# When four of the 2 MB cache copies are issued in a decoder step with two layers: from layer B into the memory attention stage

## The reference

```python
def layer_b(h, mem_k, mem_v, w_in, conv_w, ..., w_out, conv_state, delta_state):
    proj = h @ w_in
    qkv, b, a, qm, z = jnp.split(proj, ...)
    ...                                         # conv, silu, l2norm, decay
    o, S = gated_delta(q, k, v, g, beta, S0)
    o = rmsnorm(o, o_norm_w)...
    om = mem_attend(qm, mem_k, mem_v)           # softmax over 256 memory tokens, 4 heads
    branch = jnp.concatenate([o, om], axis=-1) * jax.nn.silu(z)
    return branch @ w_out, new_conv, S

# layer A, sample group, for each of the three windows (128, 512, 2048):
kc = jnp.concatenate([kbuf, k], axis=1)
keep = min(win, L + T)
return o, lse, kc[:, L + T - keep:], vc[:, L + T - keep:]
```

## Time and profile before

| what | value |
|---|---|
| median of 3 runs | 2200.28 us (2195.5 to 2202.48) |
| the profiled execution's own time | 2194.7 us |
| its span, first to last instruction | 2192.7 us |
| PE busy | 2154.7 us, 98% |
| DVE, ACT, POOL busy | 938.3, 663.8, 456.4 us |
| layer B's heads, about | 1100 to 1748 us of the span |
| memory attention stage, about | 1748 to 1963 us |
| last stage, about | 1963 to 2193 us |
| the POOL-issued DMA queue (software dynamic) | 12,000 packets, 59.73 MB |

### The profile page before, as it was taken

The page is one execution under the profiler, slowest core; times in us unless marked ns, Lnnn a source line. Parts: engine busy times, 40 slices in busy tenths (PEclk is TensorE's granted clock), DMA queues, the critical chain, the costliest instruction groups (busy, mean ns, idle before and its releaser), DMA issues.

```text
span 2192.7 us, 46735 instructions
## 1 busy us (share of the span) xinstructions
PE 2154.7 (98%) x19630; PEld 1531.5 (70%) x19630; DVE 938.3 (43%) x2431; ACT 663.8 (30%) x1589; POOL 456.4 (21%) x642
## 2 busy tenths in 40 slices
PE   8999999999999999999999999999999999999998
PEld 6888888888888876544567667676676666665444
DVE  5234354354344444321355555555555233333252
ACT  4122321312222131311234434444344344442101
POOL 0522241242123205000032322322322110020000
PEclk9999999999999999999999999999999999999999
DMA  7412211212221166666012212122110173114451
GB/s 227 154 42 64 81 30 41 78 43 67 58 59 42 35 212 227 213 207 212 13 62 93 70 74 83 67 79 80 60 53 14 40 273 97 39 59 148 136 168 53
DMA packets 210278, 210.99 MB, mean 96 GB/s; under 512 B 14262, under 2 KB 181654, under 8 KB 209151
## 3 DMA queue, kind: packets, MB, share of 16 engines
q1 hardware_dynamic: 198070, 148.27, 22.4%
q0 software_dynamic: 12000, 59.73, 7.1%
HBM read 179.56 MB, written 68.23 MB: 113 GB/s over the span
## 4 chain that ended last, share of the span: by engine, by line
PE 50%; DVE 0%; ACT 0%; issue 0%; POOL 0%; DVEq 0%
PE bank L2088 19%; PE bank L2802 8%; PE bank L3292 7%; PE bank L2146 4%; PE bank L2162 4%; PE bank L2144 2%; PE bank L2154 1%; PE bank L2818 1%; PE bank L2827 1%; PE bank L3270 1%; PE bank L3303 0%; PE bank L2177 0%; PE bank L3199 0%; PE bank L3176 0%; PE bank L2810 0%; PE bank L3186 0%
## 5 line engine op out<-in xcount | busy, mean ns | idle before, releaser
L884 PE MATMUL bank<-arena 128*128 128x256 f32 (+1 forms) x2688 | 631.7, 386 | 0.0
L884 PEld LDWEIGHTS bank<-arena 128*128 128x128 f32 x2688 | 494.5, 190 | 75.3
L2088 PE MATMUL bank<-arena 128*128 128x352 f32 x1296 | 469.2, 474 | 0.1
L2088 PEld LDWEIGHTS bank<-arena 128*128 128x128 f32 x1296 | 214.0, 190 | 58.1 <-ACT arena L2309 0.6
L2802 PE MATMUL bank<-arena 128*128 128x352 f32 x576 | 176.4, 459 | 0.0
L3292 PE MATMUL bank<-arena 128*128 128x512 f32 x360 | 167.5, 599 | 0.0
L2146 PEld LDWEIGHTS bank<-arena 128*128 128x128 f32 x864 | 125.5, 192 | 36.7 <-issue 0.3
L2802 PEld LDWEIGHTS bank<-arena 128*128 128x128 f32 x576 | 106.6, 190 | 53.3
L2162 PEld LDWEIGHTS bank<-arena 32*32 32x32 f32 x7680 | 78.8, 105 | 91.6 <-issue 39.8
L1338 POOL TENSOR_TENSOR arena<-arena 128x272 f32<-128x272 f32 (+1 forms) x48 | 31.5, 656 | 507.6 <-ACT arena L1058 487.6
L2146 PE MATMUL bank<-arena 128*128 128x128 f32 x864 | 131.3, 278 | 0.2 <-ACT arena L2329 0.2
(11 more groups left out here) (426 smaller groups left out, 2720.2 us busy)
## 6 DMA issues: line engine op xcount, KB each, us to landing
arena<-in_w_in_a SPq DMA_DIRECT2D x48, 512.0 KB, 5.1
arena<-in_w_in_b SPq DMA_DIRECT2D x40, 512.0 KB, 4.1
arena<-in_cache_win_k SPq DMA_DIRECT2D x48, 256.0 KB, 5.1
arena<-in_cache_win_v SPq DMA_DIRECT2D x48, 256.0 KB, 3.6
out<-arena SPq DMA_DIRECT2D x40, 256.0 KB, 3.3
arena<-in_w_mem_kv SPq DMA_DIRECT2D x16, 512.0 KB, 8.0
arena<-in_cache_mem_k SPq DMA_DIRECT2D x32, 256.0 KB, 4.1
arena<-in_cache_mem_v SPq DMA_DIRECT2D x32, 256.0 KB, 3.4
```

Source lines behind the costliest of these rows:

```text
L884: m = nc.tensor.matmul(o[:, 0:hi - lo], w, y, start=k == 0 and i in (0, 1, 3, 5), stop=k == KH - 1, skip_group_check=i in (2, 4, 6))
L2088: m = nc.tensor.matmul(bank[j % 3][:, 0:PART], ring.slots[:, (B1 + b) % RING, k, :], part_in(k, part_), start=k == 0, stop=k == KD - 1)
```

## The change

Copies 8 to 11 leave layer B's loop. They are now issued at the head of the memory attention stage, where copies 12 to 15 were before. Copies 12 to 15 are now issued one by one, copy 12 + s right behind the two gate products of head pair s in POOL's list. The number of transfers and bytes stays as it was, and no other engine's list is touched.

```diff
-    NUM_EARLY = 12
+    NUM_EARLY = 8
...
         copy_cache(pool, ck0, sk0, 128, DT)
         copy_cache(pool, cv0, sv0, 128, DT)
-        for n in range(NUM_EARLY, 16):
+        for n in range(NUM_EARLY, 12):
             copy_part(pool, n)
         readout(pool, NG_ - 1, "ot")
         pool.wait_ge(pr_, NPB * HB + IN_B)
         for s in range(H):
             for i in range(2):
                 after(pool, pr2d, 3 * (M_AT[(s, 2 + i)] + 1) - IN_B)
                 v = brT[:, 2 * s + i, 0:SEQ]
                 nc.gpsimd.tensor_tensor(v, v, zo_of(s, i)[:, 0:SEQ], ALU.mult).then_inc(zo2, 1)
+            copy_part(pool, 12 + s)
```

## The result

The median rises from 2198.66 to 2229.30 us (4 runs each: 2195.5 to 2202.5, and 2227.2 to 2235.8). The ratio is 1.0144, 95% interval 1.0116 to 1.0171. The forecast was 2237, range 2227 to 2250.

The account below looks back on a forecast made before the run. PE, busy 2154.7 of 2192.7 us, bounds the kernel, so any added wait counts in full. 36.9 for copy 15 plus 2 for the clock on 2200.3 gave 2239, shaded by 2 to 2237 us; range 2227 to 2250.

Parts of the forecast that it names:

- One copy holds two engines and delays what is issued beside it by its own length: DMA engines: a 2 MB copy occupies two of 16, lands after 41.2 to 42.7 us, holding up loads issued beside it.
- Step 1: Layer B: copies 8 to 11 leaving gains 0 to 0.3 us, taken as 0.
- Step 2: Memory attention stage's head: copy 12 beside block 7's load, cover 3.8 us; PE waits 0 to 4 us, taken as 0.
- Step 3: Memory attention stage: copy 13, issued at 1861.9, costs 0; loads issued meanwhile have 52 us until use.
- Step 4: Last stage's start: copy 14 makes PE wait some 6 us for keys 0 and 1, swallowed by the next step.
- Step 5: Last stage: copy 15 delays w_out_b's last block and x tile 0; unit 11 shifts 36.9 us (29.9 to 41.7).
- the allowance of 4 us for the crowd behind the copy: Last stage: loads queued on copy 15's engines take 4 us after 2009.6, so w_out_b's last block lands at 2013.6.
- Step 6: PE's clock after the last stage's wait: low granted clock costs 2 us (1.7 to 4).
- The sum: Whole kernel: 36.9 + 2 = 38.9 us on 2200.3 gives 2239, shaded by 2 to 2237 us.
- the copy is not hidden: Denies a rival for the last stage: loads pass the copy, 2200 to 2203 us, no change; chance 0.07.
- the second wait in the memory attention stage: Rival: copy 12 starts late behind another large copy, PE waits 37 us more for block 7, 2274 us; chance 0.06.
- Pieces slip through: Last stage: w_out_b passes the copy, x tile 0 sets shift of 31 to 33, 2233 to 2235 us; within forecast's 0.83.

Follow-up runs that it names:

- spread16: Changed kernel with copies 12 to 15 each issued as two 1 MB transfers of 16 rows, on 16 DMA engines: 2201.0 us, 1.0031 of the kernel before.
- small_true: Changed kernel with copies 12 to 15 in 16 KB pieces that can't be merged (last 16 bytes left out): 2230.5 us, 1.0166 of the kernel before.
- small_pieces: Changed kernel with copies 12 to 15 cut into 16 KB pieces, which by the packet counts were merged again: 2230.1 us, 1.0164 of the kernel before.
- moved_late_only: Changed kernel with copies 8 to 11 back in layer B's loop, 12 to 15 still late: 2227.5 us, 1.0149 of the kernel before.
- all_at_head: Changed kernel with copies 8 to 15 all at the memory attention stage's head, none behind gate products: 2201.1 us, 1.0036 of the kernel before.

## Why the prediction held, step by step

- *One copy holds two engines and delays what is issued beside it by its own length*: right. Share 0.13 and 55 GB/s while PE stood, as in rows 6; confirmed by spread16, and by the count of pieces and small_true for the turns. It is no fixed rule: in small_pieces, the same placement again, w_out_b got through in 29.2 us. "All of its waits in layer B's stretch are 3.9", as the prediction has it, was misread: the same answer holds 2.3 us of further waits there, for DVE and ACT, so 6.2. As nothing in layer B moved, the forecast did not suffer. The Trainium skill's account of the turns ("DMA: Bandwidth & Descriptors", "Queues, rings and completion order") agrees with this trace: 8 and 8 pieces in 10 us, and 15.1 us instead of 44.9 with quarter-size pieces.
- *Step 1, nothing from layer B*: right (moved_late_only, all_at_head).
- *Step 2, copy 12 free*: right for this kernel, and so was it that little cover is left. The reason given, that the load is ahead in its queue, does not hold by itself: in all_at_head block 7's load was issued at 1754.25 and the last four copies from 1755.01 on, and it still took 59.1 us instead of 49.6.
- *Step 3, copy 13 free*: no wait in the trace. No run moved copy 13 alone.
- *Step 4, some 6 us for the first keys, swallowed*: 4.9. Without copy 15 late it costs 8.4 in the stage, with the clock.
- *Step 5*: the mechanism and both victims were right. The term was 36.9 and measured 34.3. What was too large is the allowance of 4 us for the crowd behind the copy: w_out_b landed with the copy's end, at 2009.4 and 2009.5. The copy itself took 45.8 us from its issue, where the sum had 44.2, so part of that error was offset by another, which was luck.
- *Step 6, the clock*: 2 forecast, 2.9 measured. The row from which I took it followed a short pause; behind the long one the low clock held for nearly six microseconds of work rather than 3.4.
- *The sum*: 38.9 forecast, 37.2 in the last stage, 35.5 between the executions, 31 to 32 between medians (2229.3 - 2198.7 = 30.6; ratio 1.0144), and 33.5 for moved_late_only, whose late copies are the same. I had put the old median's distance to its profiled execution, 5.6, on top; the changed kernel's median is 0.9 below its own. That and the 4 us are why the result lies at the low end of the range.
- *The rivals*: the copy is not hidden; the second wait in the memory attention stage did not come in this kernel, but exists (5.6 and 7.3 us, not 37) when more copies start together. "Pieces slip through" came true in part in small_pieces (29.2 us) and with short pieces in small_true (15.1), and, as worked out, x tile 0 then sets about the same end.

## What to carry to other kernels

A transfer off the critical path still holds its DMA engines: ask on how many it runs and for how long, and compare that time with the cover of every load that is issued while it flies, in its own queue and in the others. Two long rows mean two engines for 40 us here. With 16 rows for each half the same 2 MB were over in 8 us, which turned a loss of 33 us into 7, or into none with the urgent loads issued first. In this last stage, which streams through few buffers, none of three moments was good for a transfer of 40 us.

## What the runs showed of the hardware that I had not expected

- SP itself was held. Its three state loads took 4.65 us to issue before; in the changed kernel SP stood at them for 41.5 us, although none of their own instructions waits on a semaphore there, and the next key was issued only at 2006.48 (timeline of SP):

```profile
1964.96 41.48 SPq L3080 DMA_DIRECT2D arena<-in_state_delta  x3
2006.48 5.25 SPq L3072 DMA_DIRECT2D arena<-in_cache_mem_k  x3
```

- The same placement in three profiled executions let w_out_b through after 44.9, 45.8 (moved_late_only) and 29.2 us (small_pieces). What decides this stays open; x tile 0 hid it from the total.
- An access pattern of 16 KB rows that lie end to end made as many packets as long rows: 210,277 in both kernels.
